# A decoder trunk with three kinds of heads: retention heads first, the gate chain over three quads, updates and two units interleaved behind a pre-norm

## The chip, the cores and the metric

The kernel runs on one core of a Trainium2 chip. The metric is the device time of one execution in microseconds; the program contains both layers of the model. Six parts of the core take part: TensorE (PE; PEld is its weight load), VectorE (DVE), ScalarE (ACT), GpSimd (POOL) and SyncE (SP) with their own instruction queues, and 16 DMA engines. Each engine runs its queue in order and waits on semaphores.

## What is computed

Two layers of a hybrid decoder. A prompt of 256 positions and 8 samples of 4 positions make T = 288 columns with 2048 model features. All is fp32. Per layer (the reference, cut):

```
h = rmsnorm(x, norm_mix_pre)
proj = einsum(h, w_in)                    # q, k, v, gate of 4 mLSTM, 4 retention, 8 gated-delta heads, and 24 gate rows
ya = sigmoid(oa) * head_norm(mlstm(qa, ka, va, gates))
yb = silu(gb) * head_norm(retention(rotary(qb), rotary(kb), vb))
yc = silu(gcz) * head_norm(gated_delta(silu(conv(q, k, v)), g, beta))
x = x + rmsnorm(concat(ya, yb, yc) @ w_out, norm_mix_post)
u = square(relu(rmsnorm(x, norm_mlp_pre) @ w_up))
x = x + rmsnorm(u @ w_down, norm_mlp_post)
```

The states of the heads, the running maxima and the last rows of the convolution are outputs too. Retention needs only constant decays. The decays of the gated-delta and mLSTM heads come from the 24 gate rows (tanh, softplus, running sums and maxima over time): the *gate chain*.

## The kernel before

**Units and quads.** Activations lie transposed, 128 features on the partitions, 16 chunks of features, 288 columns. A *unit* is 128 output features: 16 weight tiles of 128 x 128. The products keep fp32 accuracy by splitting weights and activations into a rounded fp32r part and a rest: WH, WL for weights, HH, HL (or UH, UL) for activations. Each chunk takes three matmuls of 288 columns (WH x HH, WH x HL, WL x HH), so a unit is 48 and a *quad*, four units, 192. There are 52 quads a layer: `first` (the projections of the first head), then one quad per head, in which PE multiplies the projections of the *next* head between the matrices of the present one (8 gdn, 4 ret, 4 mls, the last of them inside `out`), 4 `out`, and the MLP: 4 `up` and 4 `down` four times. `up_first` is the first of them.

**Slots.** Every engine's block walks the same list of quads (`walk`, line 251) and cuts each quad into 32 slots `t`. In slot `t` PE does three matmuls for each of two chunks of unit `t // 8` (a *turn*; `unit_part`, line 460). Tables and `if t ==` lines say in which slot an engine issues a step of a head. What stands in a slot is only an order in a queue; time comes from the semaphores.

**Weights.** SP loads a unit in four pieces into RAW[0..3]. ACT copies a piece to WH (`hi_part`), DVE subtracts it to WL (`lo_part`, line 1143). SP loads the next unit's piece when WL of this one is done. WH and WL exist twice, and the pieces of a unit wait for the matmuls of the unit before the last. The pieces of units 1 to 3 of a quad and of unit 0 of the next are issued in its odd slots, on ACT and DVE both.

**Pre-norm.** x is not scaled before the product: HH and HL are x times the gain, split; the sum of squares is built by 16 fp32 matmuls of squares (SQ, four buffers in AE) against ONES, and the factor S = rsqrt multiplies the outputs when DVE takes them from PSUM (`evac`). In `first` and `up_first` slots 0 to 7 hold the sums of two chunks each, behind the turn. ACT's `prenorm` makes HH of chunk c and the square of chunk c - 3. Before `first` comes `update_x` of the layer before (two scalings by gain and RS, one addition, for each pair of chunks): all eight pairs in `after_mlp`, then the loop's branch, then 16 times HL (`prenorm_lo`, line 1158). After `out` the two are interleaved.

**Gate chain.** 16 fp32 matmuls of the gate weights (gains multiplied in by DVE in slot 0, one operation of 128 x 2048) in slots 8 to 15 of `first`, then some 45 small operations of DVE and ACT in slots 14 to 29 of the same quad. In slot 31 PE turns the rows ROWA and ROWB into columns, waits for DVE's copies (COLA, COLB), and the rows go to DRAM, from which the head's BC is broadcast. The same quad holds `gdn_front` of the first gdn head, from slot 8: convolution, silu, l2 norms; in slots 20 and 25 PE sums the squares of q and k. All share DVE's and ACT's queues with the weight pieces.

**GpSimd** loads gate weights and constants when the layer is free (`layer_free`), and per head its parameters AUX, its rows BC and its state SIN, and stores the new state. `head` waits in order: the head before done, its state read, its new state ready, its store landed.

## Time and profile before

| | us |
|---|---|
| median of 3 runs | 3286.99 |
| lowest, highest | 3285.19, 3288.15 |
| the profiled execution | 3280.49 |
| its span in the trace | 3278.9 |
| PE busy in it | 3122.5 (95%) |
| DVE, ACT busy | 1930.1, 1535.4 |

All durations below are from the profiled execution. It is 6.5 us below the median. PE's clock was granted at 0.987 of full speed on the mean. A row of the timeline gives start, duration, engine, line, operation, what is written from what, how many of them, and in brackets how long the engine had been idle before it and whose work ended that. Matmuls overlap in the records; the distance of two starts is what one costs.

### The profile page before, as it was taken

To read this page: it belongs to the slowest core of one execution; us is meant where nothing else is said; L and a number is where in the kernel's file an instruction comes from. 1 tells how busy PE (TensorE), PEld (TensorE's weight loads), DVE (VectorE), ACT (ScalarE), POOL (GpSimd) and SP (SyncE) were. 2 spreads that over 40 slices of the span, in tenths; PEclk is the share of its full clock that TensorE was granted. 3 is DMA by queue.
4 is the path that set the end of the run, shared out by engine and by line. 5 is a ranking of instruction groups with operands and counts; after the bars stand their busy time and mean duration, and the time that the engine had idled before them with its cause. 6 is when DMAs were issued, how large, how long until landed. Compare 5 with 4: busy or idle time off the path is not lost.

```text
span 3278.9 us, 72394 instructions
## 1 busy us (share of the span) xinstructions
PE 3122.5 (95%) x23264; PEld 3057.9 (93%) x23264; DVE 1930.1 (59%) x3923; ACT 1535.4 (47%) x3564; POOL 84.5 (3%) x161
## 2 busy tenths in 40 slices
PE   5999999998999999999869999999989999999997
PEld 5989999998999999999869989999989999999997
DVE  5677755656545545455567777556665455454555
ACT  4566654544433334334446666545444333343333
POOL 0000000000000000000010000000000000000000
PEclk9999999999999999999989999999999999999999
DMA  3344455643544444544423444555435444444454
GB/s 132 128 133 135 132 162 161 185 155 110 175 166 159 164 164 166 166 160 164 151 84 121 131 132 137 168 167 177 155 118 167 165 164 167 162 163 164 163 167 147
DMA packets 266061, 499.24 MB, mean 152 GB/s; under 512 B 34272, under 2 KB 39552, under 8 KB 265664
## 3 DMA queue, kind: packets, MB, share of 16 engines
q1 hardware_dynamic: 243360, 443.56, 41.3%
q0 software_dynamic: 14496, 51.05, 4.7%
q10 hardware_dynamic: 8064, 2.80, 0.3%
q8 instruction: 82, 1.34, 0.2%
q14 instruction: 59, 0.48, 0.0%
HBM read 475.30 MB, written 22.01 MB: 152 GB/s over the span
## 4 chain that ended last, share of the span: by engine, by line
PE 79%; DVE 9%; ACT 5%; issue 4%; DMA 2%; DVEq 1%; ACTq 0%; SPq 0%; POOLq 0%; POOL 0%
PE PU L455 71%; PE PABCD L455 4%; PE PE_ L455 2%; ACT Y L787 2%; PE PF L455 2%; ACT AE L787 1%; DVE WL L1156 1%; DMA RAW<-in_w 1%; ACT WH L787 1%; DVE Y L1170 1%; PE PABCD L458 1%; DVE Y L1321 1%; DVE AE L1500 1%; DVE X L1173 0%; PE PE_ L458 0%
## 5 line engine op out<-in xcount | busy, mean ns | idle before, releaser
L455 PE MATMUL PU<-HH,WH 128*128 128x288 f32 x4096 | 1285.4, 314 | 59.3 <-DVE HL L1161 48.0
L787 ACT ACTIVATE WH<-RAW 128x512 fp32r<-128x512 f32 x1669 | 965.2, 621 | 591.9 <-PE PU L455 437.5
L455 PE MATMUL PU<-HL,WH 128*128 128x288 f32 x4096 | 1212.6, 296 | 0.0
L455 PE MATMUL PU<-HH,WL 128*128 128x288 f32 x4096 | 1208.7, 295 | 0.0
L1156 DVE TENSOR_TENSOR WL<-RAW,WH 128x512 fp32r<-128x512 f32 x1668 | 1074.5, 687 | 223.0 <-ACT WH L787 205.8
L455 PEld LDWEIGHTS PU<-HH,WH 128*128 128x128 f32 x4096 | 774.6, 189 | 79.2 <-DVE HL L1161 49.4
L455 PEld LDWEIGHTS PU<-HL,WH 128*128 128x128 f32 x4096 | 775.8, 189 | 7.0
L455 PEld LDWEIGHTS PU<-HH,WL 128*128 128x128 f32 x4096 | 775.0, 189 | 0.0
L455 PE MATMUL PU<-UH,WH 128*128 128x288 f32 x2560 | 759.0, 296 | 3.2 <-DVE UL L1310 2.0
L455 PE MATMUL PU<-UL,WH 128*128 128x288 f32 x2560 | 755.2, 295 | 0.0
L455 PE MATMUL PU<-UH,WL 128*128 128x288 f32 x2560 | 752.7, 294 | 0.0
L455 PEld LDWEIGHTS PU<-UH,WH 128*128 128x128 f32 x2560 | 479.7, 187 | 4.9 <-DVE UL L1310 2.4
L455 PEld LDWEIGHTS PU<-UH,WL 128*128 128x128 f32 x2560 | 482.1, 188 | 0.0
L455 PEld LDWEIGHTS PU<-UL,WH 128*128 128x128 f32 x2560 | 480.5, 188 | 0.1
L787 ACT ACTIVATE AE<-AE 128x288 f32<-128x288 f32 (+2 forms) x320 | 143.0, 449 | 523.4 <-DVE AE L1541 462.6
L1558 DVE TENSOR_TENSOR Y<-Y,PU 128x288 f32 (+1 forms) x96 | 43.6, 454 | 261.5 <-PE PU L455 261.5
L1541 DVE SCALAR_TENSOR_TENSOR AE<-PU,S 128x288 f32<-128x288 f32 x128 | 58.5, 457 | 235.9 <-PE PU L455 235.9
L787 ACT ACTIVATE AE<-Y 128x288 f32 (+1 forms) x64 | 28.5, 445 | 217.2 <-DVE Y L1558 122.4
L1585 DVE TENSOR_SCALAR UH<-AE 128x288 f32 (+1 forms) x128 | 39.7, 310 | 80.1 <-ACT AE L787 80.1
L787 ACT ACTIVATE Y<-SIN,BC 128x128 f32<-128x128 f32 x256 | 85.0, 387 | 0.0
L787 ACT ACTIVATE Y<-PE_ 128x256 f32<-128x256 f32 x96 | 36.6, 381 | 99.9 <-PE PE_ L458 91.1
L1500 DVE SCALAR_TENSOR_TENSOR AE<-CB,AUX,AE 128x312 f32<-128x312 f32 x144 | 77.8, 540 | 2.5
(245 smaller groups left out, 2244.4 us busy)
## 6 DMA issues: line engine op xcount, KB each, us to landing
RAW<-in_w SPq DMA_DIRECT2D x1669, 256.0 KB, 3.7
SIN<-in_sin POOLq DMA_DIRECT2D x32, 512.0 KB, 4.2
out_sout<-Y POOLq DMA_DIRECT2D x32, 512.0 KB, 5.3
BC<-gate_rows POOLq DMA_DIRECT2D x32, 304.0 KB, 4.3
AUX<-in_aux POOLq DMA_DIRECT2D x32, 152.0 KB, 3.4
X<-in_x SPq DMA_DIRECT2D x4, 576.0 KB, 7.5
out_y<-X SPq DMA_DIRECT2D x4, 576.0 KB, 2.8
Y<-in_gw POOLq DMA_DIRECT2D x2, 1024.0 KB, 5.0
```

Of the source, the lines that this page charges most:

```text
L455: return nc.tensor.matmul(out, lhsT, rhs, start=start, stop=stop, skip_group_check=True)
L458: return nc.tensor.transpose(out, in_, IDENT)
L787: return nc.scalar.activation(out, in_, f, **kw)
L1156: tt(WL[s % 2][:, k], RAW[c][:], WH[s % 2][:, k].bitcast(F32), ALU.subtract).then_inc(sem("lo_ready"), 1)
L1170: stt(Y[:, c], Y[:, c], gain[:, c:c + 1], RS[:], ALU.mult, ALU.mult).then_inc(sem("y_scaled"), 1)
L1321: tt(dec, dec, PABCD[:, :, 0:2 * HD], ALU.add).then_inc(sem("state_ready"), 1)
L1500: stt(ACC[:, c], CB[:, c, w:w + CO], tap, ACC[:, c], ALU.mult, ALU.add).then_inc(sem("gdn_taps"), 1)
L1541: stt(UPE[s % 2], psum, 0.0, S[:], ALU.max, ALU.mult).then_inc(sem("up_relu"), 1)
L1558: tt(yc, yc, psum, ALU.add).then_inc(sem("y_added"), 1)
L1585: ts(uh, UPT[s % 2], 1.0, None, ALU.mult).then_inc(sem("uh_ready"), 1)
```

## The change

It does seven things. **Order:** the four ret heads follow `first`, then 8 gdn, then 4 mls. The front of the first gdn head moves into the last ret quad. SP loads the units in that order, and the head outputs are waited for by turn (`turn_of`). **Gate chain:** its 45 steps stand in slots 10 to 21 of `first`, 1 to 28 of ret head 0 (k = 0) and 0 to 8 of ret head 1, where the turning is. The buffers move to parts of Y, CB and AE that are free then. **Gate weights** come in two halves, into the state buffer and Z[1], at the start and, for layer 1, in `out` of layer 0; DVE multiplies them in two operations of 128 x 1024. Their matmuls stand in the slots of the sums. **Update and split** are interleaved at the join of the layers too, and DVE's WL pieces of unit 1 stand between them (four pieces, behind pairs 1, 3, 5 and at the end), as ACT's WH pieces stand in `prenorm`. **Two units at once:** in `up_first` and in `first` of layer 1, even slots belong to unit 0 and odd ones to unit 1, so PE does both units' turns on each pair of chunks; sums and gate matmuls of a pair stand ahead of its turns. **Start:** the pieces of the first unit are split in the pre-norm of layer 0, with HH and HL of their chunks behind each. **Layers:** the loop over them is written out, in Python, on PE, DVE, ACT, GpSimd and SP.

```diff
+SIDE_BY_SIDE = [(t % 2, t // 2) for t in range(16)] + [divmod(t, 8) for t in range(16, SLOTS)]
...
+        GW = [SIN[:], Z[1][:].rearrange("p a t -> p (a t)")[:, 0:NC_ // 2 * HD].rearrange("p (c m) -> p c m", m=HD)]
...
-            with eng.Fori(0, DEPTH) as l:
+            for l in range(DEPTH):
...
-                quad(q0, "first", l, None, (n0, l * H_C, 0, 0, p0))
+                quad(q0, "first", l, None)
+                for k in range(H_B - 1):
+                    quad(q0 + 1 + k, "ret", l, ret_head(k))
+                quad(q0 + H_B, "ret", l, ret_head(H_B - 1), gdn_head(0, 0, 0))
...
-                with eng.Fori(0, H_B // 2) as i:
-                    for par in range(2):
-                        h = 2 * i + par
-                        quad(q0 + 1 + H_C + h, "ret", l, (n0 + H_C + h, l * H_B + h, h, par, p0 + H_C // 2 + i))
...
+        def two_at_once(kind, l):
+            return kind == "up_first" or kind == "first" and l > 0
+        def chunks_at(t, kind, l):
+            if two_at_once(kind, l):
+                return (t, t + 1) if t < 16 and t % 2 == 0 else ()
+            return (2 * t, 2 * t + 1) if t < 8 else ()
...
-                        load(c, 4 * Q + s + 1)
+                        load(c, unit + s + 1 if s < 3 else after)
...
+                with sp.Fori(0, H_B - 1) as k:
+                    next_units(q0 + k, u0 + 4 * H_C + 4 * k, u0 + 4 * H_C + 4 * k + 4)
+                next_units(q0 + H_B - 1, u0 + 4 * (H_C + H_B - 1), u0)
+                with sp.Fori(0, H_C - 1) as h:
+                    next_units(q0 + H_B + h, u0 + 4 * h, u0 + 4 * h + 4)
+                next_units(q0 + H_B + H_C - 1, u0 + 4 * (H_C - 1), u0 + 4 * (H_C + H_B))
...
-                    load_parameters(n + 1, 1 - par)
-                    load_rows(n + 1, 1 - par)
-                if next_head:
+                    load_parameters(next_at, 1 - par)
+                    load_rows(next_at, 1 - par)
                     held("state_decayed", n + 1)
                     held("state_read", n + 1)
-                    load_state(n + 1)
+                    load_state(next_at)
...
+            def load_gate_weights(l):
+                if l:
+                    held("head_done", HEADS * l + 1)
+                    held("state_decayed", HEADS * l)
+                    held("state_read", HEADS * l)
+                for j in range(2):
+                    pool.dma_start(GW[j], d["gw"][l, :, j * (NC_ // 2):(j + 1) * (NC_ // 2)]).then_inc(sem("gate_weights_in"), 16)
...
+                for k in range(H_B):
+                    if k == 2:
+                        store_rows(l)
+                    head(n0 + k, n0 + H_C + k, n0 + H_C + k + 1 if k < H_B - 1 else n0, k % 2)
...
-                s, kk = JOINED[t] if joined else divmod(t, 8)
+                s, kk = JOINED[t] if joined else SIDE_BY_SIDE[t] if two_at_once(kind, l) else divmod(t, 8)
...
-                if kind in ("first", "up_first") and t < 8:
-                    for c in (2 * t, 2 * t + 1):
+                if kind in ("first", "up_first"):
+                    for c in chunks_at(t, kind, l):
                         norm_sum(2 * l + (1 if kind == "up_first" else 0), c, c % 4, c == 0, c == NC_ - 1)
...
-            def gates(t, l):
-                if t == 8:
-                    pe.wait_ge(sem("constants_in"), 16 * len(con))
-                    pe.wait_ge(*gate("weights", l))
-                if 8 <= t < 16:
-                    for k in (2 * t - 16, 2 * t - 15):
-                        i = mm(PD[:, 0:T], GWf[:, k], X[:, k], k == 0, k == NC_ - 1)
-                    if t == 15:
-                        i.then_inc(gate("proj", 0)[0], 1)
-                if t == 31:
-                    pe.wait_ge(sem("gdn_l2_log"), 2 * (l * H_C + 1))
+            def gate_part(t, kind, l):
+                if kind == "first":
+                    for k in chunks_at(t, kind, l):
+                        if k in (0, 8):
+                            pe.wait_ge(*gate("weights_b" if k else "weights_a", l))
+                        if l == 0 and k % 4 == 0:
+                            pe.wait_ge(sem(f"x_in{k // 4}"), 16)
+                        if k % 2 == 0:
+                            pe.wait_ge(sem("x_updated"), 16 * l + k // 2 + 1)
+                        i = mm(PD[:, 0:T], GW[k // 8][:, k % 8], X[:, k], k == 0, k == NC_ - 1)
+                        if k == NC_ - 1:
+                            i.then_inc(gate("proj", 0)[0], 1)
...
+                if k == 1 and t == 8:
                     pe.wait_ge(*gate("cols", l))
...
             def quad(Q, kind, l, x, front=None, last_head=None):
                 for t in range(SLOTS):
+                    if l:
+                        gate_part(t, kind, l)
+                    norm_part(t, kind, l, x)
                     unit_part(Q, t, kind, l, x, last_head is not None)
-                    norm_part(t, kind, l, x)
+                    if not l:
+                        gate_part(t, kind, l)
+                    if kind == "ret" and x[2] < 2:
+                        gates(t, x[2], l, x)
                     mixer(t, kind, l, x)
                     if last_head:
                         mixer(t, "mls", l, last_head, last=True)
...
-                for i in range(NC_ + 3):
-                    c = i
-                    if c < NC_:
-                        if e == 0 and c % 4 == 0:
-                            act.wait_ge(sem(f"x_in{c // 4}"), 16)
-                        if c % 2 == 0:
-                            act.wait_ge(sem("x_updated"), 16 * l + 4 * e + c // 2 + 1)
+                which = e // 2
+                for g in range(NC_ // 2):
+                    if e == 0 and l == 0 and g % 2 == 0:
+                        hi_part(Q, g // 2)
+                        act.wait_ge(sem(f"x_in{g // 2}"), 16)
+                    act.wait_ge(sem("x_updated"), 16 * l + 4 * e + g + 1)
+                    for c in (2 * g, 2 * g + 1):
                         fn(HH[:, c], X[:, c], scale=gain[:, c:c + 1]).then_inc(sem("hh_ready"), 1)
-                    c = i - 3
-                    if c >= 4:
-                        act.wait_ge(sem("squares_summed"), NC_ * (2 * l + e // 2) + c - 3)
-                    if c >= 0:
+                    for c in (2 * g, 2 * g + 1):
+                        if c >= 4:
+                            act.wait_ge(sem("squares_summed"), NC_ * (2 * l + which) + c - 3)
                         fn(SQ[:, c % 4], X[:, c], ACT.Square).then_inc(sem("squares"), 1)
+                    if (e or l) and g in (1, 3, 5):
+                        hi_part(Q, g // 2 + 5)
+                if e == 0 and l == 0:
+                    for piece in range(4, 8):
+                        hi_part(Q, piece)
...
-                if t == 14:
-                    act.wait_ge(sem("gate_in"), 16 * 4 * (l + 1))
+            def gates(t, k, l):
+                if k == -1 and t == 8:
+                    act.wait_ge(sem("gate_in"), 16 * 3 * (l + 1))
...
-                if t == 17:
+                if k == -1 and t == 11:
                     act.wait_ge(*gate("biased", l))
...
-            for p in range(5):
-                hi_part(0, p)
-            walk(act, lambda l: prenorm(l, 0, NG0), quad, after_out, after_mlp)
+            walk(act, lambda l: prenorm(l, 0, NG0, l * QUADS), quad, after_out, after_mlp)
...
+            def gate_weights(l, j):
+                dve.wait_ge(sem("gate_weights_in"), 16 * 2 * (l + 1))
+                dve.wait_ge(sem("first_gain_in"), 16 * (l + 1))
+                gains = NG0[:, 8 * j:8 * j + 8].unsqueeze(2).to_broadcast([128, NC_ // 2, HD])
+                tt(GW[j], GW[j], gains, ALU.mult).then_inc(gate("weights_a", 0)[0], 1)
+            def gates(t, k, l):
+                if k == -1 and t == 10:
...
-                if t == 17:
+                if k == -1 and t == 13:
...
-                if t == 19:
+                if k == -1 and t == 19:
...
-                if t == 21:
+                if k == 0 and t == 1:
...
+                if k == 0 and t == 2:
                     dve.wait_ge(*gate("ext", l))
...
+                if k == 0 and t == 3:
...
-                if t == 24:
+                if k == 0 and t == 16:
...
-                if t == 29:
+                if k == 0 and t == 28:
...
-                if t == 31:
+                if k == 1 and t == 2:
                     dve.wait_ge(*gate("turned", l))
...
+                if kind == "down_last" and isinstance(x[1], int) and l < DEPTH - 1 and t in (9, 17):
+                    gate_weights(l + 1, t // 16)
...
-                    if t % 2:
+                    if t % 2 and not (kind in ("first", "up_first") and t < 8):
                         lo_part(Q, t // 2 + 4, l if last_head else None)
...
-                    if t % 8 == 7 and not (last_head and t == 7):
+                    if two_at_once(kind, l) and t in (8, 10):
+                        evac(Q, t // 2 - 4, kind, l, x)
+                    if t % 8 == 7 and not (last_head and t == 7) and not (two_at_once(kind, l) and t < 16):
...
+                    if kind == "up_first" and t == 15:
+                        store_up(l, x, 0)
+                        store_up(l, x, 1)
+            def update_and_split(l, which, gain, lo_l, lo_which, lo_gain, Q):
+                for g in range(8):
+                    update_x(l, which, gain, g)
+                    if g:
+                        prenorm_lo(lo_l, lo_which, lo_gain, range(2 * g - 2, 2 * g))
+                    if g in (1, 3, 5):
+                        lo_part(Q, g // 2 + 4)
+                prenorm_lo(lo_l, lo_which, lo_gain, range(14, 16))
+                lo_part(Q, 7)
+            def split_first(l):
+                if l:
+                    return
+                for c in range(4):
+                    lo_part(0, c)
+                    prenorm_lo(0, 0, NG0, range(4 * c, 4 * c + 4))
+                    if c < 2:
+                        gate_weights(0, c)
+                for piece in range(4, 8):
+                    lo_part(0, piece)
...
-                for g in range(8):
-                    update_x(l, 0, NG[:, 0], g)
-                    if g:
-                        prenorm_lo(l, 1, NG[:, 1], range(2 * g - 2, 2 * g))
-                prenorm_lo(l, 1, NG[:, 1], range(14, 16))
+                update_and_split(l, 0, NG[:, 0], l, 1, NG[:, 1], l * QUADS + HEADS + NC_ // 4)
...
-                for g in range(8):
-                    update_x(l, 1, NG[:, 2], g)
+                if l < DEPTH - 1:
+                    update_and_split(l, 1, NG[:, 2], l + 1, 0, NG0, (l + 1) * QUADS)
```

Three places in the instruction order. First DVE's queue at the end of layer 0. Before, the last two of eight updates and the branch of the loop over layers; the first HL is the second row behind the branch's target. `L1628`, `L252` are register steps.

```order
L1170 SCALAR_TENSOR_TENSOR Y<-Y,NG,RS 128x288 x2
L1173 TENSOR_TENSOR X<-X,Y 128x576
L1170 SCALAR_TENSOR_TENSOR Y<-Y,NG,RS 128x288 x2
L1173 TENSOR_TENSOR X<-X,Y 128x576
L1628 REGISTER_ALU
L252 REGISTER_ALU
L252 COMPARE_AND_BRANCH
```

And now, from the first update of that place:

```order
L1239 SCALAR_TENSOR_TENSOR Y<-Y,NG,RS 128x288 x2
L1242 TENSOR_TENSOR X<-X,Y 128x576
L1239 SCALAR_TENSOR_TENSOR Y<-Y,NG,RS 128x288 x2
L1242 TENSOR_TENSOR X<-X,Y 128x576
L1230 SCALAR_TENSOR_TENSOR HL<-X,NG0,HH 128x288 x2
L1225 TENSOR_TENSOR WL1<-RAW0,WH1 128x512
L1239 SCALAR_TENSOR_TENSOR Y<-Y,NG,RS 128x288 x2
```

The first HL moved from behind eight updates to behind two, and a WL piece of unit 1 stands behind it.

Second, PE's queue at `up_first`: the sums of the output norm, then the quad. Before, the first two turns, both of unit 0 (PU0); the `ISA` and `REGISTER_ALU` rows are waits:

```order
L455 MATMUL PABCD<-AE,ONES 128x288 x2
L466 ISA
L469 ISA
L478 REGISTER_ALU
L455 MATMUL PU0<-HH,WH0 128x288
L455 MATMUL PU0<-HL,WH0 128x288
L455 MATMUL PU0<-HH,WL0 128x288
L478 REGISTER_ALU
L455 MATMUL PU0<-HH,WH0 128x288
L455 MATMUL PU0<-HL,WH0 128x288
L455 MATMUL PU0<-HH,WL0 128x288
L455 MATMUL PABCD<-AE,ONES 128x288 x2
```

Now (the first row holds the output norm's two and the pre-norm's first two sums):

```order
L504 MATMUL PABCD<-AE,ONES 128x288 x4
L504 MATMUL PU0<-HH,WH0 128x288
L504 MATMUL PU0<-HL,WH0 128x288
L504 MATMUL PU0<-HH,WL0 128x288
L504 MATMUL PU0<-HH,WH0 128x288
L504 MATMUL PU0<-HL,WH0 128x288
L504 MATMUL PU0<-HH,WL0 128x288
L504 MATMUL PU1<-HH,WH1 128x288
L504 MATMUL PU1<-HL,WH1 128x288
L504 MATMUL PU1<-HH,WL1 128x288
```

The sums moved ahead of the turn, and six matmuls of unit 1 (PU1) follow on the same chunks.

Third, DVE's queue in `first` where the middle of the gate chain stands. Before, it is ahead of the first WL piece of unit 3 (WL1) and shares the queue with the convolution (AE<-CB):

```order
L1196 RECIPROCAL PMS<-PMS 128x288
L1197 REGISTER_ALU
L1198 TENSOR_SCALAR QKG<-PMS 64x288
L1199 TENSOR_SCALAR Z1<-PMS 32x288
L1201 REGISTER_ALU
L1202 TENSOR_SCALAR SC<-QKG 64x288
L1203 REGISTER_ALU
L1204 SCALAR_TENSOR_TENSOR PMS<-SC 128x288
L1154 REGISTER_ALU
L1156 TENSOR_TENSOR WL1<-RAW0,WH1 128x512
L1493 REGISTER_ALU
L1497 TENSOR_SCALAR AE<-CB,AUX0 128x312
```

Now, in layer 1:

```order
L1608 TENSOR_TENSOR Z0<-PU1,S 128x288
L1225 TENSOR_TENSOR WL0<-RAW1,WH0 128x512
L1265 TENSOR_SCALAR Y<-Y 64x288
L1265 TENSOR_SCALAR Y<-Y 32x288
L1267 RECIPROCAL Y<-Y 128x288
L1269 TENSOR_SCALAR Y<-Y 64x288
L1270 TENSOR_SCALAR Y<-Y 32x288
L1273 TENSOR_SCALAR Y<-Y 64x288
L1275 SCALAR_TENSOR_TENSOR Y<-Y 128x288
L1225 TENSOR_TENSOR WL0<-RAW2,WH0 128x512
```

The chain stands one unit earlier, between the second and the third WL piece of unit 2, and the convolution is gone from the quad.

## Rows read from the trace of the kernel before

**Rows 1.** The page: busy time of PE over the span.

```profile
PE 3122.5 (95%) x23264; PEld 3057.9 (93%) x23264; DVE 1930.1 (59%) x3923; ACT 1535.4 (47%) x3564; POOL 84.5 (3%) x161
```

**Rows 2.** Busy time by stretches: columns PE, PEld, DVE, ACT, POOL, clock, DMA, GB/s.

```profile
0.00:19.88 19.88, 0.00 (x0) 0.00 (x0) 5.15 (x15) 5.46 (x9) 1.89 (x7) 1.00 0.87 286
19.88:50.69 30.81, 30.81 (x160) 27.02 (x161) 17.14 (x31) 19.75 (x48) 3.25 (x6) 1.00 0.32 106
50.69:85.14 34.45, 17.69 (x110) 16.11 (x108) 27.63 (x77) 15.32 (x42) 3.54 (x7) 0.83 0.19 64
...
762.48:788.08 25.60, 25.60 (x194) 25.53 (x192) 13.65 (x24) 10.11 (x20) 0.00 (x0) 1.00 0.50 166
...
795.89:822.91 27.02, 24.14 (x128) 19.83 (x129) 21.20 (x43) 16.49 (x40) 0.00 (x0) 0.92 0.13 41
...
1650.48:1680.13 29.65, 29.64 (x160) 26.04 (x161) 16.77 (x31) 16.21 (x38) 0.34 (x1) 0.94 0.27 89
1680.13:1714.57 34.44, 18.43 (x110) 17.08 (x109) 27.60 (x77) 15.32 (x42) 3.54 (x7) 0.80 0.19 64
```

**Rows 3.** PE's waits, whole span: total us, times, longest.

```profile
PE PU L455 <- DVE HL L1161: 48.0, 4, 19.9
PE PE_ L455 <- ACT AE L787: 33.3, 16, 11.1
...
PE PU L455 <- DVE COLB L1281: 6.1, 2, 3.0
```

**Rows 4.** The same stretches view for four head quads: gdn, gdn, last gdn, ret.

```profile
85.14:130.95 45.81, 44.38 (x326) 42.90 (x327) 29.75 (x75) 27.82 (x80) 3.54 (x7) 0.94 0.39 129
...
354.49:399.10 44.61, 42.11 (x329) 40.41 (x327) 32.30 (x80) 30.18 (x89) 2.17 (x5) 1.00 0.42 132
399.10:440.17 41.07, 40.34 (x324) 39.51 (x323) 24.77 (x58) 23.93 (x67) 2.40 (x5) 1.00 0.45 145
...
473.12:506.90 33.78, 33.09 (x248) 31.86 (x247) 19.48 (x38) 16.15 (x38) 2.16 (x4) 1.00 0.57 172
```

**Rows 5.** Timeline at the start, ACT and PE.

```profile
6.50 0.63 ACT L787 ACTIVATE WH<-RAW 128x512 fp32r<-128x512 f32 x1 [4.22 <-DMA RAW<-in_w]
...
18.22 0.63 ACT L787 ACTIVATE WH<-RAW 128x512 fp32r<-128x512 f32 x1 [3.67 <-DMA RAW<-in_w]
...
19.88 0.61 PE L455 MATMUL PU<-HH,WH 128*128 128x288 f32 x1 [19.88 <-DVE HL L1161]
```

**Rows 6.** Timeline of PE in `first`, one block of sums and the next.

```profile
27.01 1.13 PE L455 MATMUL PABCD<-AE,ONES 128*128 128x288 f32 x4
...
28.77 1.13 PE L455 MATMUL PABCD<-AE,ONES 128*128 128x288 f32 x4
```

**Rows 7.** DVE's busy time in three stretches of the gate chain.

```profile
54.98:59.13 4.15, 3.93 (x8) 1.00 0.05 19
64.90:69.10 4.20, 3.97 (x17) 0.70 0.18 62
82.10:84.56 2.46, 2.23 (x10) 0.82 0.52 139
```

**Rows 8.** Timeline of DVE at the join of the layers.

```profile
1633.21 0.95 DVE L1170 SCALAR_TENSOR_TENSOR Y<-Y,NG,RS 128x288 f32<-128x288 f32 x2 [2.34 <-ACT RS L787]
...
1649.91 3.52 DVE L1161 SCALAR_TENSOR_TENSOR HL<-X,NG,HH 128x288 fp32r<-128x288 f32 x8 [3.41 <-issue]
```

**Rows 9.** Timeline of DVE ahead of `up_first`.

```profile
792.01 0.95 DVE L1170 SCALAR_TENSOR_TENSOR Y<-Y,NG,RS 128x288 f32<-128x288 f32 x2 [2.36 <-ACT RS L787]
...
795.32 0.94 DVE L1161 SCALAR_TENSOR_TENSOR HL<-X,NG,HH 128x288 fp32r<-128x288 f32 x2
...
797.83 0.94 DVE L1161 SCALAR_TENSOR_TENSOR HL<-X,NG,HH 128x288 fp32r<-128x288 f32 x2
...
812.26 0.69 DVE L1156 TENSOR_TENSOR WL<-RAW,WH 128x512 fp32r<-128x512 f32 x1
```

**Rows 10.** Timeline of DVE in the second ret quad, ahead of the rotation.

```profile
478.50 0.31 DVE L1287 TENSOR_SCALAR GATE<-GATE 128x288 f32<-128x288 f32 x1 [2.44 <-ACT GATE L787]
```

214 lines of the change are left out of this document (116 added, 98 removed).

## The prediction

> **What bounds the kernel now.** I read the page's busy line first, then PE's waits, then busy time by stretches cut at the first matmul of each quad, then timelines inside the short stretches. PE is busy 95% of the span [rows 1], so only its idle time, its half-clock time and its own added work can move the end. A quad without a head takes 25.60 us (762.48 to 788.08) at clock 1.00 with PE never idle: 192 matmuls at 0.133 us, 6.40 a unit [rows 2]. Everything beyond that sits in three kinds of place. (a) The first quad of each layer: 30.81 + 34.45 us in layer 0, 29.65 + 34.44 in layer 1, for 25.6 us of unit work [rows 2]; behind it stand a start at 19.88, a wait of 11.1 us on the squares of the front of the first gdn head, and a half-rate clock after it (0.83 in the stretch) [rows 2, 3]. (b) The join of the layers and the two pre-norms after `out`; HL is the longest of PE's waits, 48.0 us in 4 [rows 3]. (c) The head quads, where PE runs 42.1 of 44.6 us in gdn and 33.1 of 33.8 in ret [rows 4]; their mathematics does not change. DVE and ACT matter only where they end a wait of (a) and (b).
>
> **Layer 0, units 0 and 1.** Today ACT splits piece 0 at 6.50, but after four pieces it asks for a fifth whose load was queued behind the constants, and stands until 18.22, ahead of the whole pre-norm; so PE starts at 19.88 [rows 5]. The change puts HH and HL behind each piece. The first piece would be ready at 6.5, but 1 MB of gate weights now shares the transfers. They moved 286 GB/s at a share of 0.87 in 0 to 19.88 [rows 2], so 1 MB costs up to 3.7 us: piece 0 at 8.5 to 9, piece 3 at 17 instead of some 14. One PE turn (two chunks) is a block of two fp32 sums with six matmuls, 28.77 - 27.01 = 1.76 us, of which the block is 1.76 - 6 x 0.133 = 0.96 [rows 6]. With the gate matmuls in the same turn there are two blocks back to back, some 1.71 + 0.80 = 2.51. PE starts at about 10.5 and waits in turn 0 for the gate weights (DVE has four HL and one 1.15 us half of today's 2.29 us multiplication ahead, so 13.7); then seven turns and part of them at the lower clock, 18.6, to 32.3; unit 1 with 6.4 and no sums, 38.7. I take 39 against 50.69 today: **-11.7**. Bounds: 35 if nothing collides, 45 if gate weights land only after all of SP's first loads (they saturate until about 18 us).
>
> What the Trainium skill says here stands apart: "DMA: Bandwidth & Descriptors", section Queues, rings and completion order, has each DMA engine alternate between the queue rows that have work. By it the gate weights, on GpSimd's row, would take every other turn and be in near 10 us, which gives 39; a strict order behind SP's loads would give the 45. No row of before shows the two rows competing with a large transfer on each.
>
> **Layer 0, units 2 and 3.** Today 34.45 us [rows 2]. The front of a gdn head leaves this quad, and with it the 11.1 us wait; the turning of the gate rows and the wait for its copies (PE 3.0 us behind 2.46 us of DVE) go to ret head 1 [rows 3, 7]. The chain's first part (4.15 us, with the reciprocal [rows 7]) stands ahead of the third WL piece of unit 2. In layer 0 the sums are ready a unit earlier (S near 32, PE needs that piece at 39 + 3.2), so it is covered by unit 1. I take 12.8 + 0.2: **-21.4**. If the cover is gone, 4.
>
> **The join.** DVE starts its updates at 1633.21 and does all eight before the first HL, which comes at 1649.91, 3.41 us of it at the loop's branch [rows 8]. Straight code has no such branch, and HL(0) comes after two updates, as in `up_first` today: update at 792.01, HL at 795.32, PE at 795.89, so +3.88 [rows 9]. PE starts at 1637.1 instead of 1650.48. Its first pair (12 matmuls at the lower clock, each at most twice 0.133) takes some 2.9; seven further pairs take 1.71 for gates and sums plus 12 x 0.133, or 3.31 each: 23.2. DVE needs 2.51 a pair (795.32 to 797.83) and 0.65 for a WL piece in four of eight pairs, 2.83, so PE is the slower one here. Units 0 and 1 end at 1663.2 against 1680.13: **-16.9**.
>
> **Layer 1, units 2 and 3.** Now there is no spare unit: the last sum, S, evacuation 0 and WL come one after another when units 0 and 1 end nearly together. Ln and Exp 0.95, evacuation 0.45, WL 0.65 put unit 2 some 0.8 late, its second piece 0.3. Then DVE waits for tanh's three ACT operations (1.36) and runs the 4.15 us chain ahead of the third piece, which arrives 7.8 after the end of unit 1 where PE wants it at 4.3: 3.5. In all 12.8 + 4.6 = 17.4 against 34.44: **-17.0**. Bounds for the stall: 0 to 8 (the chain and tanh twice over).
>
> **The two pre-norms after out.** Today units 0 and 1 take 27.02 us from 795.89 [rows 2]. In pairs, PE wants 0.96 + 1.60 = 2.56 per pair, DVE 2.83, so DVE is the bound. HL of the last pair is ready at 796.2 + 6 x 2.51 + 3 x 0.65 + 0.9 = 814.1, the last WL piece of unit 1 at 814.8; PE then has a turn of unit 1, a block, and two turns, to 818.2; S, evacuation and WL put unit 2 at 819.0 against 822.91: -3.9 each, **-7.8**. The four WL pieces that move in front (today the first at 812.26 [rows 9]) are why it is not the 6.4 us of a whole unit. SP only reloads RAW earlier.
>
> **What is given back.** Ret head 0 gets 4.20 us of DVE chain [rows 7] before its rotation. DVE idles 2.44 us there for the gate's exponential [rows 10], and the rest delays the transposes: +1.2, and +0.2 for ACT. Ret head 1 gets the turning on PE, 1.1, and copies of 2.46 which fit into that 2.44: +1.4. Ret head 3 gets the front; among gdn heads it is worth 44.61 - 41.07 = 3.5 [rows 4], its PE work alone 1.0; I take 3.2. The first gdn quad (45.81) loses its wait for BC and becomes 44.6 like the others: -1.2 [rows 4]. That is +5 a layer, **+10**. Bounds 2 to 14 a layer, the upper one if the 10.8 us of chain in the three rows of [rows 7] and 3.5 of front all show. Off the path: gate weights for layer 1 are loaded in `out` and multiplied in `down_last`, 2.3 us on a DVE that is busy 13.65 of 25.60 us [rows 2]; I price it at 0, with 1 for a late weight piece. GpSimd's `store_rows` stands ahead of ret head 2's hand-over and holds the parameters of ret head 3 for some 7 us of a 33.8 us quad: 0. The order of projections, and SP's with it, moves no bytes.
>
> **Sum.** -11.7 - 21.4 - 16.9 - 17.0 - 7.8 + 10 + 1 = -63.8. Against its own execution, 3280.5 us, that is 3216.7. The median of before is 3287.0, 6.5 above that execution; I keep the difference and predict **3223 us**.
>
> **Rivals.** *The chain stays on the path.* For it: DVE's queue is in order, and every piece of the chain stands ahead of a WL piece or a rotation. Against it: 19.5 busy of 33.8 us in ret [rows 4]. If half of the bounds above shows in both layers (9 more in heads, 3 in layer 1's stall, for two layers 18 + 3), the time is 3223 + 21 = 3244. *Start starved by the gate weights:* 6 to 10 late, 3223 + 8 = 3231; for it the share of 0.87, against it the 106 GB/s of the stretch behind it [rows 2]. *Turns don't pay:* the change would not do what it says if DVE remained the bound with no gain, since PE only waits in another place; then the pre-norms give 0 and the join 3 less, 3234. *Slower than before:* fetching the longer, straight code. The one row of it is the 3.41 us at the branch [rows 8]. The program has both layers written out, and if fresh code stalled PE like that at every quad boundary of the 104, from the 19th on (63.8 / 3.4) the gain would be lost; 25 give 3308. Against it: in the straight ret and `out` code of today PE shows no such idle time, so I give it little.
>
> **How the numbers follow.** Forecast 0.60; chain 0.17; start 0.10; turns 0.06; a larger gain, if the stall of layer 1 and the give-back are near their lower bounds (3223 - 4 - 6 = 3213), 0.04; slower 0.03. The range of 3206 to 3248 takes in the first four and the bounds of the start and the stall. A measurement here tells 0.2% (6.6 us) from no change: faster 0.95, same 0.02, slower 0.03.
>
> **What would show it.** The first PE matmul near 10 us and unit 2 of layer 0 near 39; PE at 1.00 clock without the 11 us hole; a quad `first` of about 25 + 13 us in layer 0; in layer 1 a restart 3.9 us after the first update, unit 2 some 31 us after that, with one wait of 3 to 4 us on WL; unit 2 of `up_first` 23 us after its first matmul instead of 27; ret 0, 1 and 3 at 34.4, 35.2 and 37. Wrong: a first matmul after 14, HL still 5 us or more per pre-norm pair, or ret quads above 38.

## The result, and the profile after

| | before | after |
|---|---|---|
| median of the runs, us | 3286.09 (3284.32 to 3288.15) | 3250.85 (3250.09 to 3252.01) |
| span of the profiled execution, us | 3278.9 | 3250.5 |

The ratio is 0.9893, with a 95% interval of 0.9876 to 0.991: 35 us faster, where 64 were forecast (3223 us, range 3206 to 3248). The direction was right, the size by the medians about half, and the time lies 3 us above the range. From span to span the difference is 28.4 us: the profiled execution of before lay 6.5 us under its median, that of after (3252.0 us) 1.2 us above its own.

The stretches of after, cut as those of before in [rows 2]: the start, units 0 and 1 and units 2 and 3 of layer 0's first quad, units 0 and 1 of its `up_first`, then both halves of layer 1's first quad. Columns as there.

```profile
0.00:10.94 10.94, 1.65 (x5) 1.25 (x5) 4.61 (x15) 4.89 (x10) 1.96 (x7) 1.00 0.80 266
10.94:42.90 31.96, 30.51 (x159) 26.22 (x157) 17.73 (x31) 18.58 (x42) 5.82 (x11) 1.00 0.62 213
42.90:55.70 12.80, 12.80 (x99) 12.80 (x97) 9.27 (x19) 4.99 (x9) 0.00 (x0) 1.00 0.52 163
...
786.48:808.93 22.45, 21.39 (x127) 19.57 (x125) 18.80 (x38) 14.12 (x34) 0.00 (x0) 0.93 0.14 47
...
1624.77:1653.04 28.27, 27.21 (x155) 23.92 (x153) 18.30 (x37) 13.58 (x32) 4.76 (x9) 0.98 0.25 82
1653.04:1671.18 18.14, 14.90 (x96) 14.43 (x97) 13.50 (x26) 7.99 (x15) 0.00 (x0) 0.91 0.52 158
```

These are the stages that the change is about. With what the heads give back they gained 57 us, where 64 were forecast. The larger loss is elsewhere, in a stage that was priced at zero. The same view for the second gdn head of layer 0, the first unit of the third, the rest of that quad, and the first unit of the fourth:

```profile
242.14:286.62 44.48, 42.13 (x329) 40.41 (x327) 32.32 (x80) 30.17 (x89) 2.23 (x5) 1.00 0.42 132
286.62:305.70 19.08, 13.27 (x84) 12.71 (x82) 9.06 (x25) 8.76 (x28) 1.31 (x3) 0.82 0.44 124
305.70:339.05 33.35, 31.94 (x248) 30.45 (x247) 23.31 (x56) 21.39 (x61) 0.83 (x2) 1.00 0.31 103
339.05:350.12 11.07, 10.16 (x83) 9.93 (x82) 8.57 (x24) 8.78 (x28) 1.33 (x3) 1.00 0.64 186
```

The first unit takes 19.08 us with as many instructions as the 11.07 us one. It is so in four of sixteen gdn quads: the third and the fifth head of each layer, 52.43, 51.71, 52.83 and 51.65 us (from the first matmul of a quad's first unit to that of the next quad) against 45.01, 44.98, 44.98 and 44.97 for the same heads in before. That is 28.7 us, 6.7 to 7.9 a quad. These heads are where the `Fori` over pairs of gdn heads, which both kernels have, begins its second and its third pass. ScalarE's timeline there in layer 0 (start, us, operation, idle time before and its releaser), then VectorE's in layer 1:

```profile
289.24 0.63 ACT L852 ACTIVATE WH<-RAW 128x512 fp32r<-128x512 f32 x1 [0.67 <-ACT CNEW L852]
294.38 0.31 ACT L852 ACTIVATE Y<-Z 128x128 f32<-128x128 f32 x1 [4.51 <-issue]
294.60 0.89 ACT L852 ACTIVATE Y<-BC,CUR 128x128 f32<-128x128 f32 x3
298.52 0.44 ACT L852 ACTIVATE Y<-Y 128x288 f32<-128x288 f32 x1 [3.04 <-issue]
...
1904.96 0.46 DVE L1385 TENSOR_TENSOR UL<-AM,UH 128x288 f32 x1
1911.61 0.69 DVE L1225 TENSOR_TENSOR WL<-RAW,WH 128x512 fp32r<-128x512 f32 x1 [6.20 <-issue]
```

"issue" says that nothing in the profile was waited for. 294.38 is the first operation of the loop's body. TensorE waits 5.8 us for these two engines, and its clock falls to 0.82 over the unit (0.74 in layer 1, 1900.29 to 1919.79). Its waits in 286 to 305 us (total, times, longest):

```profile
PE PABCD L507 <- DVE Y L1505: 3.1, 1, 3.1
PE PABCD L507 <- ACT Y L852: 2.7, 1, 2.7
```

The DMA view of this stretch of after, and that of 165 to 350 us of before, in which the same loop jumps back twice:

```profile
q1 hardware_dynamic: 716, 1.31, 26.7%
q0 software_dynamic: 272, 0.99, 15.5%
q10 hardware_dynamic: 144, 0.04, 0.9%
q14 instruction: 4, 0.03, 0.5%
```
```profile
q1 hardware_dynamic: 9523, 17.33, 29.4%
q0 software_dynamic: 1664, 6.06, 9.8%
q10 hardware_dynamic: 1152, 0.43, 0.9%
```

After fetches four packets of instructions, 8 KB each, at 291.92, 292.23, 297.06 and 299.20 us: two inside ScalarE's first gap, one inside its second. In layer 1 packets start at 1906.63 and 1909.74, inside VectorE's gap. Before fetches none in its stretch, so its loop's code was still there.

Not every "issue" gap is code. Before shows eight more on ScalarE in its mls heads, of 3.0 to 3.3 us (the first ends at 600.65); there ScalarE issues two stores to DRAM inside the gap. The gaps above have no DMA issue in them.

### The profile page after: what moved, and what is told of

It reads as the page before. It is cut to its first block, busy times and chain, and to the rows that moved or that the text cites. A ratio compares the mean times of both kernels' runs of the same rounds, so it can differ in the third digit from the quotient of the medians.

```text
span 3250.5 us, 69571 instructions
## 1 busy us (share of the span) xinstructions
PE 3127.6 (96%) x23264; PEld 3065.0 (94%) x23264; DVE 1926.4 (59%) x3926; ACT 1531.8 (47%) x3564; POOL 85.3 (3%) x163
## 4 chain that ended last, share of the span: by engine, by line
PE 79%; DVE 8%; ACT 6%; issue 4%; DMA 2%; DVEq 0%; ACTq 0%; POOL 0%; SPq 0%; POOLq 0%
PE PU L504 71%; PE PABCD L504 4%; ACT Y L852 2%; PE PE_ L504 2%; DVE WL L1225 2%; ACT AE L852 2%; PE PF L504 2%; DMA RAW<-in_w 1%; ACT WH L852 1%; PE PABCD L507 1%; DVE Y L1396 1%; DVE AE L1575 1%; PE PE_ L507 0%; DVE AM L1501 0%; DVE PMS L1373 0%
## 5 line engine op out<-in xcount | busy, mean ns | idle before, releaser
L852 ACT ACTIVATE AE<-AE 128x288 f32<-128x288 f32 (+4 forms) x322 | 143.1, 447 | 517.3 <-DVE AE L1616 456.1
L852 ACT ACTIVATE AE<-Y 128x288 f32 (+1 forms) x64 | 28.4, 444 | 217.0 <-DVE Y L1633 123.0
L852 ACT ACTIVATE Y<-PE_ 128x256 f32<-128x256 f32 x96 | 36.6, 381 | 106.3 <-PE PE_ L507 91.1
```

What stands on the lines that cost most here:

```text
L852: return nc.scalar.activation(out, in_, f, **kw)
```

## Experiments: who stands still

Every kernel below was timed beside before, whose medians in the three sessions of measurement were 3283.8, 3282.3 and 3283.6 us. Three theories: the gaps are code being fetched (A), GpSimd, which loops there too, loads late (B), or the new order of the work makes these quads long (C).

**straight**: the loop is written out, on GpSimd in the same way.
```diff
-                with eng.Fori(0, H_C // 2 - 1) as i:
+                for i in range(H_C // 2 - 1):
                     gdn_pair(i, False)
...
```


> The kernel after, with the three passes of the loop over pairs of gated delta heads written out as straight code on every engine; nothing else differs, and the work and its order are the same. Theory A (code): in the trace of after the first quad of the second and of the third pass has a first unit of 18.4 to 19.5 us where all others have 11.1; ScalarE stands 4.5 + 3.0 us and 5.3 + 1.3 us for nothing but issue there in layer 0, VectorE 6.2 and 5.5 us in layer 1, and 8 KB packets of the instruction queue land in just these gaps. Then straight code takes away all four: 4 x 7.3 to 8.4 us = 31 us, so 3219.5 us (3216 to 3223), every such unit at 11.1 us and no issue gap over 1 us on ScalarE and VectorE. Theory B (loads): the loads of the next head's rows by GpSimd, which also loops there, come late; then the writing out of the others alone gives nothing, but this kernel can't tell it from A, since GpSimd's loop is written out too. Theory C (the order of the work, such as a collision of the later state loads with the head's start, makes these quads long): 3250.9 us, as after.

Measured 3216.3 us, ratio 0.9798 (0.9782 to 0.9814). ScalarE and VectorE have no issue gap over 0.5 us left, and gdn quads take 43.96 us, also the third and the fifth (the first and the last of the eight differ, there as in before). C is out.

**pe_pool_straight**: written out on TensorE and GpSimd, looped on ScalarE and VectorE.

> The kernel after, with the same loop written out on TensorE and GpSimd only; ScalarE and VectorE keep it. Theory A (code of ScalarE and VectorE): nothing changes, 3250.9 us (3248 to 3253), the four first units of 18.4 to 19.5 us and the issue gaps stay. Theory B (GpSimd's loop delays the loads of the next head's rows, and with them ScalarE): the four gaps go, 3219.5 us.

Measured 3251.2 us, 0.9907 (0.9889 to 0.9925), the four gaps in place (3.9 + 2.2 us and 4.9 + 1.8 us on ScalarE, 5.9 and 5.7 us on VectorE). B is out, and so is TensorE's own loop: it is the code of ScalarE and VectorE.

## Experiments: why this loop and not the one of before

Both kernels loop over the same body. I counted the instructions of the built programs, register arithmetic and waits included (two waits on semaphores make one instruction), and laid them beside the packets. In before ScalarE's instructions 190, 318, 446 and 574 run at 96.03, 137.91, 359.14 and 402.76 us, and packets start at 96.06, 137.79, 359.40 and 404.31: one 8 KB packet each 128 instructions. By the trace's own records the last two are 448 and 579, so this holds to within five. ScalarE does not stand at these places, so the packet that it enters is already there and the one that starts lies ahead. The place of the count against the packets is not in the traces: I took some 66 instructions ahead of the code on ScalarE and some 53 on VectorE. That choice fits the runs below and is bounded by them to 66 to 71 and 40 to 55. With it the loop's body lies so, in instructions and in packets of 128:

| kernel, layer, engine | begins, ends | packets | fetches |
|---|---|---|---|
| before, ScalarE | 233, 502 | 1 to 3 | no |
| before, VectorE | 286, 598 | 2 to 4 | no |
| after, 0, ScalarE | 378, 640 | 2 to 5 | yes |
| after, 0, VectorE | 408, 705 | 3 to 5 | no |
| after, 1, ScalarE | 1686, 1955 | 13 to 15 | no |
| after, 1, VectorE | 2045, 2355 | 15 to 18 | yes |

The bodies are 262 to 312 instructions long (between two jumps back the traces have 266 to 312 records: VectorE's as here, ScalarE's four more, as many as it issues DMAs there); what differs is how they lie. The change writes the layers out and moves heads and the gate chain ahead of the loop, so its place shifts by an amount nobody chose. This gives a theory that can be tried from both sides (A1), against the one that any jump back costs in code that is written out by layer (A2).

**padded**: after, loops kept, with 16 instructions more (32 waits that are long met) ahead of each loop that fetches. The cut shows ScalarE's; VectorE has the same for `l == 1`.
```diff
+                    if kind == "ret" and x[2] == 0 and l == 0 and t % 2:
+                        act.wait_ge(sem("ones_set"), 1)
+                        act.wait_ge(sem("ones_set"), 1)
```


> The kernel after with all its loops, and 32 waits that are long met (16 instructions) on ScalarE in the retention head before layer 0's loop, and as many on VectorE in the one before layer 1's loop. They only move the loop's code 16 instructions further on. Theory A1 (where the body lies): the trace has an 8 KB packet of code each 128 instructions of an engine, and the loops that fetch nothing when they jump back (both engines in before, VectorE in layer 0 and ScalarE in layer 1 of after) end two such packets behind the one they begin in, while the two that fetch would end three behind: ScalarE's body in layer 0 overhangs by an instruction or so, VectorE's in layer 1 begins 3 instructions ahead of a packet's end. 16 instructions further on both lie on three packets: the four gaps go, 3220 us (3217 to 3224). Theory A2 (any jump back in this kernel costs a fetch, since the code before and behind it is longer than in before): 3251 us, and a little more for the waits.

Measured 3220.7 us, 0.9809 (0.9792 to 0.9825). With sixteen instructions added to each of two engines after is 30 us faster, by its own median and by that of pe_pool_straight in the same session. The four quads take 44.89, 44.86, 44.83 and 44.83 us. ScalarE at the head of layer 0's second pass:

```profile
285.11 0.63 ACT L852 ACTIVATE WH<-RAW 128x512 fp32r<-128x512 f32 x1 [0.67 <-ACT CNEW L852]
285.65 0.29 ACT L852 ACTIVATE Y<-Z 128x128 f32<-128x128 f32 x1
285.85 0.89 ACT L852 ACTIVATE Y<-BC,CUR 128x128 f32<-128x128 f32 x3
286.77 0.44 ACT L852 ACTIVATE Y<-Y 128x288 f32<-128x288 f32 x1
```

The same four groups as in after, without a gap. A2 is out.

**before_padded** and **before_pad10**: before, with 32 or 20 waits (16 or 10 instructions) ahead of ScalarE's first work.
```diff
             act.wait_ge(sem("ones_set"), 1)
+            for _ in range(32):            # before_pad10: 20
+                act.wait_ge(sem("ones_set"), 1)
```


> The kernel before, with 32 waits that are long met (16 instructions) on ScalarE ahead of its first work; nothing else. By theory A1 ScalarE's loop over pairs of gated delta heads, whose body ends 10 or so instructions ahead of a packet's end, then ends three 8 KB packets behind the one it begins in, and each jump back fetches: two in each layer, each some 7.3 to 8.4 us, so 3286 + 29 to 34 = 3315 to 3320 us, with issue gaps of 4 to 8 us on ScalarE at the start of the third and the fifth of these heads in both layers. Theory A2 (jumps cost only in the kernel with its layers written out): 3286 us (3284 to 3289). No theory gives less.

Measured 3295.2 us, 1.0037 (1.0024 to 1.005). The body now ends at 518, in packet 4, and all four gaps are there, but of 3.3 to 3.9 us, with at most 0.7 us more behind them, and the quads lose 2.5 to 4.1 us, not 7.3 to 8.4. Those two figures were first units of 18.4 to 19.5 us less 11.1; counted as here, quad against the same quad of before, after loses 6.7 to 7.9. Right on the place, wrong on the price.

> The kernel before with 20 long met waits (10 instructions) ahead of ScalarE's first work, where before_padded had 16 instructions. By the count, the body's last instruction (446 of the code, and some 66 ahead of it) is then the first, or one of the first six, of its fourth 8 KB packet, as in layer 0 of after, and not the seventh as in before_padded. Theory S (the price is high in after because the engine enters the new packet only with its very last instruction, asks for the one behind it, and then has to wait for that before it gets the code it jumps to): gaps of 7 us, 4 x 7.5 us, so 3314 us (3308 to 3320). Theory T (a jump costs 3.3 to 3.9 us of gap wherever the body ends, and the rest in after has another cause): as before_padded, 3295 us. Theory U (the body still fits, since the count is off by an instruction or more): 3284 us.

Measured 3298.5 us, 1.0046 (1.0029 to 1.0062). The first gaps of before_padded and of before_pad10:

```profile
181.24 0.31 ACT L787 ACTIVATE Y<-Z 128x128 f32<-128x128 f32 x1 [3.34 <-issue]
```
```profile
183.49 0.31 ACT L787 ACTIVATE Y<-Z 128x128 f32<-128x128 f32 x1 [4.57 <-issue]
```

U is out. The time is near T's 3295 and far from S's 3314. Of S a part holds in the trace: with the end at 512 the four gaps are 3.9 to 5.2 us, near the first gaps of after (4.5 and 5.3), and the quads lose 2.4 to 5.7 us; the totals of the two kernels, 1.0037 and 1.0046 with intervals that overlap, do not tell them apart. The second gap in after (3.0 and 1.3 us) came once, with 0.55 us. Its cause stays open; in after the body begins 6 instructions ahead of a packet's end, here 13, and 7 in before_padded, where the second gap is 0.57 us.

**before_dve30** and **before_dve60**: the same on VectorE with 30 and 60 instructions (60 and 120 waits), to try the rule on the other engine with a number given ahead.

> The kernel before with 30 instructions of long met waits ahead of VectorE's first split, in a time in which VectorE waits for ScalarE anyway. By the count that after and padded bound (what stands ahead of the code is 40 to 55 instructions on VectorE: with 1992 the loop of layer 1 begins just ahead of a packet, with 2008 behind it), VectorE's loop over gated delta pairs now begins at 303 to 318 and ends at 615 to 630, within the packets 256 to 639: no fetch at a jump back, 3282 us (3280 to 3286). If it is any shift of the code that costs: 3295 us or more.

> As before_dve30 with 60 instructions. The body now begins at 333 to 348 and ends at 645 to 660, three packets on: a fetch at each of the four jumps back, with issue gaps of 3 to 6 us on VectorE at the third and the fifth gated delta head of both layers. In after such a gap on VectorE cost 7.3 to 8.4 us of a quad, ScalarE's of 3.3 to 3.9 us in before_padded 2.5 to 4.1; so 4 x 3 to 8 us: 3294 to 3314 us, 3304 taken. If the place of the body decides nothing on VectorE: 3282 us.

Measured 3284.1 us, 1.0004 (0.9994 to 1.0014), and 3304.6 us, 1.0069 (1.0052 to 1.0086). Thirty instructions cost nothing, sixty 21 us; the four quads lose 4.8 to 5.2 each. In before_dve60 VectorE stands at the jump in layer 0:

```profile
183.36 0.69 DVE L1156 TENSOR_TENSOR WL<-RAW,WH 128x512 fp32r<-128x512 f32 x1 [3.51 <-issue]
277.81 0.69 DVE L1156 TENSOR_TENSOR WL<-RAW,WH 128x512 fp32r<-128x512 f32 x1 [3.33 <-issue]
```

So in every loop looked at a body that ended two packets behind its first jumped back without a fetch, and one that ended three behind fetched. The Trainium skill ("Runtime: NRT & Kernel Launch", section Instruction fetch mechanics) has an instruction memory of 512 instructions that fills in sequence, and a taken branch whose target isn't in it wait for a DMA. The runs agree with that, if one of four packets of 128 is the one being fetched ahead: three are left for the loop. That section also has blocks of 16 KB, 256 instructions, for all engines. The traces have 8 KB packets for ScalarE and VectorE, and the difference decides here: in blocks of 256 ScalarE's body in layer 0 lies on the same two in after and in padded, and only after fetches. The section's preference for written-out loops is borne out in part only:

**before_straight**: before with the loop written out on TensorE, ScalarE and VectorE.

> The kernel before with the loop over pairs of gated delta heads written out on TensorE, ScalarE and VectorE; nothing else. If the 35 us between after and its straight version are what loops of this kind cost anywhere, it gains 30 us: 3254 us. If only the fetches cost, and before has none at these jumps, what goes is the arithmetic on registers: in straight a gated delta quad takes 43.96 us against 44.45 to 44.89 in padded, some 4 us in each layer, so 3284 - 8 = 3276 us (3272 to 3280), and the 3.4 us gap at the layer loop stays.

Measured 3281.5 us, 0.9995 (0.9985 to 1.0004): no difference. The gdn quads give 2.4 and 2.8 us a layer, less than expected, and the first `out` quad takes 40.5 and 39.4 us where it took 36.6 and 36.5. Where there is no fetch, writing out wins little. In that `out` quad TensorE waits 1.9 us for VectorE's queue at a place where before has 0.6 to 0.7 us, and in layer 0 its clock over the quad is 0.92 where it was 1.00; why VectorE is later there stays open.

## Experiments: what the turns are worth

**no_turns_up**: straight, units 0 and 1 of `up_first` one after the other; their stores move with them (not shown).
```diff
-            return kind == "up_first" or kind == "first" and l > 0
+            return kind == "first" and l > 0
...
```


> The kernel straight, but behind the second pre-norm of each layer its first two units follow one another as in before; the chunk by chunk update and the early pieces stay, as do the turns at the start of layer 1. In straight units 0 and 1 take 11.4 + 11.1 = 22.5 us there, paced by VectorE; one after the other, unit 0 is paced by VectorE to the last chunk at some 21 us, and unit 1 then runs whole, 6.4 to 7.6 us: 27.5 to 29 us, so 5 to 6.5 us more in each layer, 3216.3 + 11.5 = 3228 us (3224 to 3230). Rival: unit 0 is done earlier when it needn't share TensorE, and what is gained there makes up for half of it: 3222 us. That the turns give nothing: 3216 us.

Measured 3221.2 us, 0.9811 (0.9794 to 0.9827). Unit 0 takes 18.65 and unit 1 6.40 us; the two stretches of straight, then of this kernel (units 0 and 1, units 2 and 3):

```profile
764.36:786.82 22.46, 21.26 (x127) 19.21 (x125) 18.81 (x38) 14.11 (x34) 0.00 (x0) 0.95 0.15 47
786.82:799.69 12.87, 12.87 (x97) 12.87 (x98) 9.54 (x19) 6.50 (x12) 0.00 (x0) 1.00 0.59 183
```
```profile
766.30:791.35 25.05, 22.41 (x127) 19.15 (x126) 20.49 (x40) 15.02 (x35) 0.00 (x0) 0.94 0.24 76
791.35:804.14 12.79, 12.79 (x98) 12.79 (x97) 7.95 (x16) 5.06 (x10) 0.00 (x0) 1.00 0.45 145
```

The quad is 2.5 us longer without the turns (37.84 and 37.85 for 35.33), half of what I expected: unit 0 alone is done 2.4 us earlier than the 21 I gave it. The rival, with 3222 us, was the nearer one.

**no_turns_first**: straight, with the turns kept at `up_first` and dropped in layer 1's first quad.

> The kernel straight, but in layer 1's first quad units 0 and 1 follow one another, with the gate projection and the sums of squares of two chunks ahead of each step of unit 0 as in layer 0; the turns at the second pre-norms stay. In straight units 0 and 1 take 28.1 us there. In turn unit 0 is paced by VectorE to about 26 us and unit 1 adds 6.4 us whole: 32.5 us, 4.4 us more (3 to 6.4), so 3220.7 us (3219 to 3223). Rival: TensorE is the one that is late there, with the projection among its work, and the turns move nothing but its waits: 3216 to 3217 us.

Measured 3209.05 us, 0.9779 (0.9762 to 0.9795): 7 us faster, where I expected 4 slower and the rival none. The first quad of layer 1 takes 39.74 us, not 46.28. Layer 1 in straight and in this kernel, units 0 and 1 in two stretches, then unit 2:

```profile
1602.12:1616.68 14.56, 14.56 (x82) 12.79 (x81) 14.38 (x29) 9.47 (x23) 0.00 (x0) 0.97 0.17 55
1616.68:1630.26 13.58, 12.53 (x74) 10.99 (x73) 4.37 (x9) 4.71 (x11) 4.76 (x9) 1.00 0.35 109
1630.26:1642.00 11.74, 8.49 (x48) 8.03 (x49) 8.97 (x18) 5.19 (x11) 0.00 (x0) 0.85 0.45 146
```
```profile
1602.47:1623.01 20.54, 20.54 (x106) 17.45 (x105) 16.92 (x34) 11.50 (x29) 4.07 (x8) 0.98 0.21 63
1623.01:1629.41 6.40, 6.40 (x50) 6.40 (x49) 4.66 (x8) 4.01 (x9) 0.67 (x2) 1.00 0.76 263
1629.41:1635.81 6.40, 6.40 (x50) 6.40 (x49) 5.30 (x12) 2.07 (x4) 0.00 (x0) 1.00 0.40 131
```

TensorE is busy nearly throughout units 0 and 1 in both: with the gate projection among its work it is the slower engine, and turns have no waits to fill. Of the 6.5 us, 5.3 lie in unit 2. Turns end both units together, so both weight buffers are in use to the end, and unit 0's evacuation, the chain and unit 2's pieces all come at once; which of these weighs most was not tried. From straight, TensorE's wait in this stage, VectorE's order around it, and the clock after it (0.44 us a matmul for 0.29):

```profile
PE PU L504 <- DVE WL L1225: 4.2, 2, 3.2
```
```profile
1633.08 1.95 DVE L1267 RECIPROCAL Y<-Y 128x288 f32<-128x288 f32 x1
...
1636.45 1.89 DVE L1225 TENSOR_TENSOR WL<-RAW,WH 128x512 fp32r<-128x512 f32 x3
```
```profile
1637.19 0.61 PE L504 MATMUL PU<-HH,WH 128*128 128x288 f32 x1 [3.17 <-DVE WL L1225]
1637.60 0.44 PE L504 MATMUL PU<-HL,WH 128*128 128x288 f32 x1
```

The wait of 3.17 us is at unit 2's third piece. One after the other, unit 1's 6.4 us stand between, and in the trace both waits are gone. Retention head 0 gives 2.2 us back (37.42 for 35.20).

**padded_no_turns_first**: the same on padded.

> The kernel padded (loops kept, moved by 16 instructions) with units 0 and 1 one after the other in layer 1's first quad. no_turns_first gained 7.3 us against straight, where TensorE waits 4.2 us for weight pieces of unit 2 with turns and not at all without; the same here: 3220.7 - 7 = 3213.5 us (3211 to 3217). If the gain came from ScalarE's or VectorE's code and not from the turns: 3220 us.

Measured 3216.6 us, 0.9802 (0.9786 to 0.9819), 4 us less than padded; the quad takes 39.75 us for 45.84, the same 6 us in another build. The intervals of each of these pairs overlap, so it is the stage in the trace that carries this finding. no_turns_first is the fastest kernel of the study.

## Why the prediction missed

The forecast's terms, and what the two profiled executions show for each, us:

| term | forecast | measured |
|---|---|---|
| layer 0, units 0 and 1 (end at 50.69, now 42.90) | -11.7 | -7.8 |
| layer 0, units 2 and 3 | -21.4 | -21.7 |
| join, units 0 and 1 of layer 1 | -16.9 | -13.2 |
| layer 1, units 2 and 3 | -17.0 | -16.3 |
| two pre-norms after `out` | -7.8 | -7.1 |
| given back in the heads, and the late piece | +11 | +9.0 |
| third and fifth gdn head of each layer | 0 | +28.7 |
| sum | -63.8 | -28.4 |

**The step that failed** is first of all none of the sum's terms but what it left out, 28.7 of the 35.4 us that are missing; the other 6.7 are terms that were mis-sized, above all the start of layer 0 (3.9) and the join (3.7). The work of the gdn heads was taken to cost the same since none of it changed, and that its loop stood at another place in the code was given no price. The forecast did have code fetching as its slower rival, from the gap of 3.41 us at the layer's branch [rows 8], and read it wrongly: it tied the cost to new straight code, at quad boundaries, where the trace of straight has no such gap on ScalarE or VectorE. The row it rested on was a jump back, with an 8 KB packet that starts at 1647.98, inside the gap. What it held against the rival was TensorE's record in "straight ret and `out` code", but the ret quads and three of the four `out` quads of before are loops, and the engines that stand in after are the other two. Read as a jump back, the question would have been which jumps back are left and where each loop's code comes to lie, and before had the warning: by the count above ScalarE's loop ends there 10 instructions ahead of a packet's end. With the fetches taken away the change gains nearly what was forecast: padded is 63 us under the before of its session, 60.3 from span to span. None of the forecast's signs of being wrong came (the first matmul of unit 0 at 10.94, 2.5 to 3.1 us from one pair's HL to the next in the pre-norm of `up_first`, no ret quad above 37.1); none of them looked at the gdn loops.

**Layer 0's start.** First matmul of unit 0 at 10.94, forecast 10.5; right. Units 0 and 1 took 31.96 us, forecast 28.5. TensorE waits 1.4 us for the gate weights (their matmuls start at 14.44, forecast 13.7) and is busy 30.5, so most of it is its own work: a turn takes 2.73 us (16.07 to 18.80 in straight), where I had put it together from 1.71 and 0.80. Over eight turns that is 1.8 of the 3.5 us. The rest is not in every run: in after the first block of gate matmuls and the sums behind it take 2.08 and 1.52 us, in padded 1.08 and 0.75, and padded's two units take 30.3 us in all; what makes that block slow in one run and not in the other stays open. The weights landed 8.2 and 10.4 us after issue, with X on the other queue at 9.1 where four such loads were under way: neither queue waited for the other to be done, so the forecast's 45, by which SP's loads all go first, is out. The Trainium skill ("DMA: Bandwidth & Descriptors", section Queues, rings and completion order) has the engines alternate between queues, and this agrees with it.

**Layer 0, units 2 and 3**: 12.80 us at clock 1.00 without a wait, 21.7 less than [rows 2] has. The largest term, and right because its removal left nothing that was late next.

**The join.** TensorE starts on unit 0 5.5 us after the first update, forecast 3.9; before took 17.3. From after:

```profile
1619.32 0.95 DVE L1239 SCALAR_TENSOR_TENSOR Y<-Y,NG,RS 128x288 f32<-128x288 f32 x2 [2.40 <-ACT RS L852]
```
```profile
1621.21 2.26 PE L504 MATMUL PABCD<-X,SIN 128*128 128x288 f32 x4 [2.93 <-DVE X L1242]
1623.26 2.13 PE L504 MATMUL PABCD<-AE,ONES 128*128 128x288 f32 x4
1624.77 0.85 PE L504 MATMUL PU<-HH,WH 128*128 128x288 f32 x1
```

The 3.9 were taken from `up_first`, which has no gate matmuls ahead of its turns; here the first pair's gates and sums stand there for 3.6 us. So the restart is 11.8 us earlier, forecast 13.4, and units 0 and 1 take 28.27, forecast 26.1. The stall of unit 2 on its third weight piece was forecast at 3.5 us and is 3.2. But it was booked as the price of having no spare unit. The forecast did not ask whether the turns, which take the spare unit away, were worth that; without them the quad is 6.5 us shorter, of which the next one gives 2.2 back.

**Pre-norms**: 35.32 and 35.30 us for 39.82 and 39.81, less 0.9 and 1.0 us more in the `out` quads ahead of them. The gain was put down to turns and chunked updates together; no_turns_up shows the turns to be 2.5 of the 4.5.

**Given back**: retention heads 0 and 3 at 37.1 and 35.7 us in layer 0, 34.8 and 35.7 in layer 1, forecast 34.4 and 37; the sum came near by errors that cancel. The rival in which the chain stays on the path speaks of half of the bounds, but its 9 us more a layer are the whole way from 5 to the bound of 14, so its 3244 us was the outer case.

**From execution to median.** I added the 6.5 us by which the median of before stood over its profiled execution. After's stands 1.2 us under its own. Such a difference belongs to one execution, and carrying it over put the forecast that much higher: without it 3216.7 us, 34 under the result and not 28. That padded's 3220.7 us come so near to 3223 is in part this luck.

## What to carry to other kernels

Where a change adds or moves code ahead of a loop, look in the trace for instruction packets and for issue gaps at each loop's jump back, count the instructions of its body on each engine and where they begin, and either keep the body within the packets that stay or write it out; sixteen idle instructions were worth 30 us here. In the two places tried, side by side turns paid where the engine waited for its input (2.5 us) and cost where it was busy itself (6.5 us), since they end two units at once and uncover what the second one hid. When a stage's work does not change, say also why its place in the code does not matter.

## What the chip showed that was not expected

- A loop's price depends on where its code lies: much the same body jumped back for nothing, or for 2.4 to 7.9 us of a quad of 45.
- ScalarE and VectorE fetch code in 8 KB packets of 128 instructions, while the other instruction queue's packets are 16 KB. Loops of 262 to 312 instructions stayed resident when they ended two 8 KB packets behind their first, and not three behind.
- A jump back that fetches leaves ScalarE or VectorE standing for 3.3 to 6.2 us in the gdn loops, in after on ScalarE with a second gap of 1.3 to 3.0 us; in after TensorE's clock also fell over such a unit, to 0.82 in layer 0.
